# Encoder layer with PEER experts, one core: 48 late tokens leave the feature matmuls in place of 32

## The reference, cut to what matters

```python
def peer_layer(x, w_q, keys1, keys2, u_tab, v_tab):
    q = (xt @ w_q).reshape(T, PEER_HEADS, 2, half)
    s1 = jnp.einsum('thd,hnd->thn', q[:, :, 0], keys1)
    s2 = jnp.einsum('thd,hnd->thn', q[:, :, 1], keys2)
    v1, i1 = lax.top_k(s1, PEER_TOPK)
    v2, i2 = lax.top_k(s2, PEER_TOPK)
    ...                                  # the 16 best of v1 + v2: eidx, sc
    gate = jax.nn.softmax(sc, axis=-1)
    u = jnp.take(u_tab, eidx, axis=0)
    a = jnp.einsum('nhkd,nd->nhk', u, x)             # "features"
    w = jax.nn.gelu(a, approximate=False) * gate
    return jnp.einsum('nhk,nhkd->nd', w, jnp.take(v_tab, eidx, axis=0))
x = layer_norm(DN_ALPHA * x + peer_layer(x, ...), ln2_g, ln2_b)
```

## Time and profile before

| | |
|---|---|
| timed executions | 1432.85, 1434.01, 1437.87 us, median 1434.01 |
| profiled execution | 1433.48 us, its span 1431.8 us |
| TensorE, VectorE, GpSimd, ScalarE busy | 98%, 76%, 63%, 42% of the span |
| feature matmuls (three lines, 128 tiles) | 3072 of 352 columns |
| features begin, sums begin | 349.16 us, 893.5 us |
| DMA in the 60 us from 700, in the 100 us from 1000 | 416 GB/s, 369 GB/s |

### The profile page before, as it was taken

How to read it: one execution, slowest core, us unless ns; L and a number is a source line. 1 busy time by engine, 2 the same in 40 slices (tenths; PEclk the granted TensorE clock), 3 DMA queues, 4 the chain that set the end, 5 groups by cost and what they waited for, 6 DMA issues and landing times.

```text
span 1431.8 us, 24761 instructions
## 1 busy us (share of the span) xinstructions
PE 1406.7 (98%) x8045; PEld 1248.2 (87%) x8045; DVE 1087.3 (76%) x2324; ACT 606.7 (42%) x1019; POOL 903.4 (63%) x595
## 2 busy tenths in 40 slices
PE   9999999999999999999999999999999999999996
PEld 5888878888999999999999999878888888888885
DVE  5366666688999998858774885987777777777786
ACT  5666751324333354454544443333333333333332
POOL 3422331335599978979888786766666666666744
PEclk9999999999999999999999999999999999999998
DMA  6213120423689979999999899999999999999981
GB/s 243 75 50 113 59 90 1 147 84 102 197 316 342 323 259 395 417 389 418 418 417 399 341 381 407 383 388 387 371 374 374 372 366 360 367 368 366 372 315 59
DMA packets 138959, 415.41 MB, mean 290 GB/s; under 512 B 13904, under 2 KB 56656, under 8 KB 136720
## 3 DMA queue, kind: packets, MB, share of 16 engines
q1 hardware_dynamic: 80128, 240.69, 45.9%
q0 software_dynamic: 42064, 151.15, 26.8%
q10 hardware_dynamic: 16704, 22.81, 4.3%
HBM read 363.89 MB, written 50.14 MB: 289 GB/s over the span
## 4 chain that ended last, share of the span: by engine, by line
PE 76%; DVE 8%; DMA 5%; POOL 4%; issue 3%; ACT 2%; SPq 1%; DVEq 0%; ACTq 0%; POOLq 0%
PE banks L2019 12%; PE banks L2021 11%; PE banks L2020 11%; PE banks L1964 11%; PE banks L1965 11%; PE banks L1966 11%; DMA raw<-v_tab 3%; POOL lo L501 2%; PE banks L2081 2%; PE banks L2237 1%; PE banks L2238 1%; POOL rows L822 1%; PE banks L2174 1%; DMA rows<-u_rows,expert_at 1%; DVE rows L1454 1%
## 5 line engine op out<-in xcount | busy, mean ns | idle before, releaser
L501 POOL TENSOR_TENSOR lo<-raw,hi 128x1024 fp32r<-128x1024 f32 x224 | 540.2, 2413 | 416.5 <-ACT hi L495 396.5
L1964 PE MATMUL banks<-x1T_hi,hi 128*128 128x352 f32 (+3 forms) x1168 | 389.9, 334 | 1.3 <-ACT kept L1106 1.0
L1965 PE MATMUL banks<-x1T_lo,hi 128*128 128x352 f32 (+3 forms) x1168 | 384.6, 329 | 0.0
L1966 PE MATMUL banks<-x1T_hi,lo 128*128 128x352 f32 (+3 forms) x1168 | 383.6, 328 | 0.0
L495 ACT ACTIVATE hi<-raw 128x1024 fp32r<-128x1024 f32 x291 | 305.6, 1050 | 57.0 <-DMA raw<-u_t 37.4
L2019 PE MATMUL banks<-hi,wgt_hi 128*128 128x512 f32 x750 | 292.1, 389 | 2.0 <-DVE wgt_lo L1811 1.9
L2020 PE MATMUL banks<-lo,wgt_hi 128*128 128x512 f32 x750 | 291.8, 389 | 0.0
L2021 PE MATMUL banks<-hi,wgt_lo 128*128 128x512 f32 x750 | 291.8, 389 | 0.0
L1964 PEld LDWEIGHTS banks<-x1T_hi,hi 128*128 128x128 f32 x1168 | 219.8, 188 | 6.2 <-ACT kept L1106 1.3
L1966 PEld LDWEIGHTS banks<-x1T_hi,lo 128*128 128x128 f32 x1168 | 220.3, 189 | 4.4
L1965 PEld LDWEIGHTS banks<-x1T_lo,hi 128*128 128x128 f32 x1168 | 220.1, 188 | 3.9
(11 more groups left out here) (245 smaller groups left out, 1846.7 us busy)
## 6 DMA issues: line engine op xcount, KB each, us to landing
raw<-u_t SPq DMA_DIRECT2D x128, 512.0 KB
raw<-v_tab SPq DMA_DIRECT2D x128, 512.0 KB
g_scratch<-stage SPq DMA_DIRECT2D x12, 2048.0 KB
gelu_scratch<-gelu ACTq DMA_DIRECT2D x116, 192.0 KB
ga<-gelu_scratch SPq DMA_DIRECT2D x29, 768.0 KB
gg<-g_scratch SPq DMA_DIRECT2D x14, 1536.0 KB
raw<-w SPq DMA_DIRECT2D x26, 512.0 KB
raw<-w_pq SPq DMA_DIRECT2D x16, 512.0 KB
```

The costliest lines, as they stand in the source:

```text
L501: eng.tensor_tensor(l[:, :], raw[:, c % RAW_SLOTS, :], h[:, :].bitcast(F32), ALU.subtract).then_inc(odd_lo_ready if by_vector(c) else lo_r ...
L1964: pe.matmul(o, h[:, s], hiT[:, k, tokens], start=(k == 0), stop=False)
L1965: pe.matmul(o, h[:, s], loT[:, k, tokens], start=False, stop=False)
L1966: ins = pe.matmul(o, l[:, s], hiT[:, k, tokens], start=False, stop=(k == KT - 1))
```

## The change

The late tokens are 48 and not 32, as a set of 32 (the last ones) and a set of 16. The feature matmuls have 336 columns and not 352, and gelu scratch in DRAM has 336 columns. The late tokens need 48 gathers and not 32. The number of u rows gathered in the feature phase stays 144, because 16 more rows of block 0 (`EXTRA` 32) go into the sums, where octets 2 to 5 take three each and the other octets up to 13 two; their gelu and gates are applied in two batches. Expert numbers, gates and weights of the late tokens are turned by way of DRAM, two stores and two loads each, and the second set's x goes through DRAM too (eight copies) and gets a home of its own: VectorE and ScalarE change homes four times in place of three. Six groups in the last pair are scattered in three parts, and not four. The chosen experts are turned one tile later (`CHOSEN_AT`), the gathers for late tokens start one tile later (`LATE_ROWS`), the first 16 late dots are spread differently (`FIRST_DOTS`). The 1.0 in the columns past the dense ones is written into the two load buffers `ga` once, and not into the gelu buffers. A load of gelu scratch now fills 336 of 384 columns of each of four rows of a partition. Four `gelu` buffers of 336 columns and `small` with 192 columns keep the buffers behind them at multiples of 256 bytes.

```diff
-LATE_TOKENS = 32
-SPREAD = P // LATE_TOKENS
+LATE_SETS = (32, 16)
+LATE_TOKENS = sum(LATE_SETS)
 LATE_AT = P - LATE_TOKENS
-LATE_RANKS = RANKS // SPREAD
+LATE_RANKS = sum(RANKS // (P // n) for n in LATE_SETS)
+LATE_MOVES = len(LATE_SETS)
 FEATURED = DENSE - LATE_TOKENS
-EXTRA = 16
+EXTRA = 32
+EXTRA_BATCHES = (16, 16)
...
-LATE_ROWS = (0, 0, 0, 2, 3, 3, 2, 2, 2, 2, 2, 2)
+LATE_ROWS = (0, 0, 0, 0, 2, 3, 3, 3, 3, 2, 2, 2)
+FIRST_DOTS = (0, 2, 2, 2, 2, 3, 2, 3)
+assert sum(FIRST_DOTS) == 2 * ROWS
...
+CHOSEN_AT = 1
+FIRST_BATCH_AT = 8
...
-    a_dram = nc.dram_tensor("gelu_scratch", (ETILES // 4, P, 4, DENSE), F32, kind="Internal").ap()
+    a_dram = nc.dram_tensor("gelu_scratch", (ETILES // 4, P, 4, FEATURED), F32, kind="Internal").ap()
+    turn_dram = [[nc.dram_tensor(f"{what}_scratch{i}", (P // n, n, n), dt, kind="Internal").ap()
+                  for i, n in enumerate(LATE_SETS)]
+                 for what, dt in (("late_number", U32), ("late_gate", F32), ("late_weight", F32))]
+    second_dram = nc.dram_tensor("second_scratch", (P // LATE_SETS[1], LATE_SETS[1], D), F32, kind="Internal").ap()
...
+        idle_gelu = ExitStack()
+        extra.append(sb("extra2", [P, D], F32, idle_gelu))
+        idle_gelu.close()
+        gelu = [sb(f"gelu{i}", [P, FEATURED]) for i in range(GELU_SLOTS)]
...
-        small = sb("small", [P, P])
+        small = sb("small", [P, P + 64])
...
-        late_parts = row_weight[:, LATE_TOKENS:].bitcast(BF16).rearrange("p (m t two) -> p m t two", m=3, two=2)
+        late_parts = sel[:, 0, :, :].rearrange("p b n -> p (b n)")[:, 0:3 * LATE_TOKENS].bitcast(BF16).rearrange(
+            "p (m t two) -> p m t two", m=3, two=2)
+        late_x_second = sel[:, 0:2, :, :].rearrange("p m b n -> p (m b n)")
...
-            used_by = n // 2 if n < len(late_slots) else WHOLE_GROUPS + (n - len(late_slots)) // 3
+            if n < len(late_slots):
+                used_by = n // 2 - (HOT_SLOTS if n // 2 >= WHOLE_GROUPS else 0)
+            else:
+                used_by = WHOLE_GROUPS + (n - len(late_slots)) // 3
...
-        EXTRA_ASKED_AT, EXTRA_DOT_AT = (2, 4), (5, 7)
-        def extra_rows(j, par, at):
-            if isinstance(j, int) and j == 0:
-                return {k: (2 * par + i, i) for i, k in enumerate(at)}
-            return {at[1]: (2 * j + (2 + par), par)}
+        ASKED_AT = {2: (2, 4), 3: (0, 2, 4)}
+        DOT_AT = {2: (4, 6), 3: (2, 4, 6)}
+        def extra_number_of(i, each, q):
+            return (2 * i + (EXTRA_BATCHES[0] - 12 + q) if each == 2 else 3 * i + (q - 2)) if not early_extras(i) else 2 * i + q
...
+            sp.dma_start(second_dram.rearrange("g t d -> t g d"),
+                         x1[LATE_AT:LATE_AT + LATE_SETS[1], TB - 1, :].unsqueeze(1).to_broadcast(
+                             [LATE_SETS[1], P // LATE_SETS[1], D])).then_inc(second_stored, 16)
...
+            def store_numbers():
                 sp.wait_ge(late_numbers_ready, 1)
-                for g in range(SPREAD):
-                    sp.dma_start(late_numbers[late_group(g), :],
-                                 block_numbers[LATE_AT:, late_group(g)]).then_inc(late_numbers_moved, 16)
-            def move_gates():
+                for i, n, tokens, columns in late_sets():
+                    sp.dma_start(turn_dram[0][i].rearrange("g t c -> t g c"),
+                                 block_numbers[tokens, :].rearrange("t (g c) -> t g c", c=n)
+                                 ).then_inc(late_numbers_stored, 16)
+            def load_numbers():
+                sp.wait_ge(late_numbers_stored, 16 * LATE_MOVES)
+                for i, n, tokens, columns in late_sets():
+                    sp.dma_start(late_numbers[:, columns], turn_dram[0][i].rearrange("g t c -> (g t) c")
...
+            def load_second_x():
+                sp.wait_ge(selT_ready, 2)
+                sp.wait_ge(second_stored, 16)
+                sp.dma_start(late_x_second, second_dram.rearrange("g t d -> (g t) d")).then_inc(second_x_moved, 16)
...
+                    if first and t == 6:
+                        load_gates_turned()
+                    if first and t == 8:
+                        load_second_x()
+                    if weights and t == 0:
+                        store_weights()
+                    if weights and t == 2:
+                        load_weights()
...
-            for k in range(2):
+            for k in range(3):
                 load_features(k, A_PRE // 4 - 1)
-            move_numbers()
-            for k in range(2, 4):
-                load_features(k, A_PRE // 4 - 1)
+            store_numbers()
+            load_features(3, A_PRE // 4 - 1)
+            load_numbers()
             two_chunks(0, first=True)
             two_chunks(1)
             two_chunks(2)
-            move_weights()
-            with sp.Fori(3, O_MID) as o:
-                two_chunks(o)
+            two_chunks(3)
+            two_chunks(4, weights=True)
...
-                    sp.dma_start(ga[slot][:, :, :], a_dram[g]).then_inc(comb_loaded[slot], 16)
+                    sp.dma_start(ga[slot][:, :, 0:FEATURED], a_dram[g]).then_inc(comb_loaded[slot], 16)
...
+                    if k in ASKED_AT[each]:
+                        q = ASKED_AT[each].index(k)
+                        extra_number(extra_number_of(2 * j + par, each, q), q)
                     first = U_ROWS + par * ROWS + k + AHEAD
                     gather(v_rows, [first, first + 1], o, (S_V + 8 * par + k, 2 * o))
-                    if k in extras:
-                        extra_row(extras[k][1])
+                    if k in ASKED_AT[each]:
+                        extra_row(q)
...
+            v_octet(0, 0, 2)
+            v_octet(0, 1, 2)
+            for slot in range(GELU_SLOTS):
+                pool.wait_ge(gelu_stored[slot], 16 * (A_PRE + A_MID) // GELU_SLOTS)
+            with pool.Fori(1, 3) as i:
+                v_octet(i, 0, 3)
+                v_octet(i, 1, 3)
+            with pool.Fori(3, OCTETS // 2 - 1) as i:
+                v_octet(i, 0, 2)
+                v_octet(i, 1, 2)
...
-                act.activation(gelu[k][:, 0:FEATURED] if keep is None else kept[:, keep, 0:FEATURED],
+                act.activation(gelu[k][:, :] if keep is None else kept[:, keep, 0:FEATURED],
...
+            def second_home():
+                act.wait_ge(second_x_moved, 16)
+                act.wait_ge(row_used, R_PRE * ROWS + LATE_SETS[0])
+                home(late_x_second)
...
-                        if first and tile == 0:
+                        if first and tile == CHOSEN_AT:
...
                         if second and tile == 0:
+                            second_home()
+                        if third and tile == 0:
...
-            for slot in range(GELU_SLOTS):
-                dve.memset(gelu[slot][:, FEATURED:DENSE], 1.0).then_inc(ones_ready, 1)
...
+                    if homes is not None and tile == 0:
+                        dve.wait_ge(homes_ready, homes)
+                    done = sum(FIRST_DOTS[:tile]) if first else 2 * tile
+                    for n in range(done, done + (FIRST_DOTS[tile] if first else 2)):
...
-            two_chunks(0, first=True)
+            two_chunks(0, homes=3, first=True)
             two_chunks(1)
-            two_chunks(2, second=True)
+            two_chunks(2, homes=4)
+            two_chunks(3, homes=5)
...
+            for slot in range(2):
+                dve.memset(ga[slot][:, :, FEATURED:DENSE], 1.0).then_inc(ones_ready, 1)
...
+                    if k in DOT_AT[each]:
+                        q = DOT_AT[each].index(k)
+                        n = extra_number_of(i, each, q)
+                        extra_dot_of(n, q, i + 1 if q < 2 else i - 1)
...
+            def weigh_extras(batch):
+                dve.wait_ge(dots_gelu_ready, 2 + batch)
+                weigh_rows(slice(FIRST_EXTRA + sum(EXTRA_BATCHES[:batch]),
+                                 FIRST_EXTRA + sum(EXTRA_BATCHES[:batch + 1]))).then_inc(row_weight_ready, 1)
+                dve.wait_ge(row_weight_ready, 2 + batch)
```

More of the change, by code:

```diff
@@ L647, in two_chunks @@
+            def two_chunks(o, first=False, weights=False):
                 for t in range(MID_TILES):
@@ L1109, in gelu_tile @@
                 if keep is None:
-                    if first and k == 0:
-                        act.wait_ge(ones_ready, GELU_SLOTS)
                     act.wait_ge(gelu_ready, 4 * it + (k + 1))
@@ L1750, in _, with two_chunks @@
             one_hots(0, 0, True)
-            def two_chunks(o, first=False, second=False, last=False):
+            def two_chunks(o, homes=None, first=False, last=False):
                 for tile in range(8):
```

150 lines of the change are left out of this document (86 added, 64 removed).

## The result

The changed kernel takes 1441.51 us, the median of 7 runs (1437.50 to 1443.99), the kernel before 1434.01 in its 7 runs: a ratio of 1.0051, 95% interval 1.0030 to 1.0072. It is slower by 7.5 us, where 1427.5 was forecast, and lies above the range. The profiled execution took 1438.85 us, 5.4 more than that of before.

A forecast was written before the change was run, and what follows sets the result against it. TensorE, busy for 98% of the span, was taken as the bound. Gains and losses of 1.4 + 7.4 - 0.3 - 2.5 = 6.0 us took the profiled 1433.48 us to 1427.5 us, range 1419 to 1439.

The forecast's parts named there:

- Term 1: Feature matmuls: 16 columns fewer gain 0.157 us a tile, 20.1 us over all 128 tiles; bounds nothing and 22.5 us.
- Terms 2 and 3: Up to the first scatter, and late numbers by way of DRAM: together one gain, 1.4 us, with GpSimd as bound.
- the side chance named: Before the first scatter: a 2.30 us conversion may take 1 us or less, bringing the scatter 1.3 us earlier.
- Term 4: Feature tiles 57 to 103: 47 x 0.157 = 7.4 us gained, with DMA transfers fitting.
- The second stop of VectorE: Tiles 57 to 103: second late-token block adds a 9.8 us stop, GpSimd's lead falls to about 2 us, costed at nothing.
- The turned gates, weights and x lie beside other work: Feature phase: nobody waits for these moves within a pair of chunks, so they cost nothing.
- the mean over a pair: Over a pair of chunks: DMA needs 50.3 us at 416 GB/s, TensorE 51.9 us, so it fits by 1.6 us.
- Term 5: Last pair of chunks: 3.8 us gained, 0.9 lost to more matmuls, 3.2 to waiting for VectorE's products: -0.3 us.
- Term 6: Expert sums: 16 more row gathers cost 1.5 us there and 1 us at their start; bounds 0 and 15.
- The rival that held for slower: Expert sums become DMA-bound: loss of 14 us and not 2.5, total 1439.0 us; chance 0.14.
- One or two more dots on VectorE in the 32.7 us of an octet fit: Expert sums: VectorE, busy for three quarters, could take two more dots even at 3.29 us.
- The 1 us that the sum put at the start of the sums: Where the expert sums begin, with the feature stretch's DMA behind them: a loss of 1 us.

The follow-up runs named there:

- q3: Kernel before with 336-column feature matmuls and gelu (16 tokens' gelu left out) and the gates' parts in PSUM, nothing else added: 1422.15 us.
- c2: Changed kernel with each extra dot cut from 1024 columns to 64, gathers whole: 1432.07 us, ratio 0.9987.
- t5: Changed kernel with extra dots on odd tiles in octets with two, and only two of three late products made on VectorE: 1428.03 us.
- p2: Changed kernel with gates' parts in PSUM, extra dots on odd tiles in octets with two, second x loaded in the second pair of chunks: 1426.24 us.
- a1: Changed kernel with the second x's load moved from the first pair of chunks into the second: 1440.38 us, ratio 1.0046.
- c1: Changed kernel with the extra rows' dots one tile later in each octet, on odd tiles: 1441.53 us, ratio 1.0051.
- d1: Changed kernel with extra dots on odd tiles (5 and 7) in octets with two, unchanged in octets with three: 1436.56 us, ratio 1.0002.
- d2: As d1, and the second x is loaded in the second pair of chunks: 1434.06 us, ratio 0.9998.
- p1: Changed kernel with the three parts of the 48 late tokens' gates copied once into PSUM and read from there: 1432.08 us, ratio 0.9990.
- q2: Changed kernel with gates' parts in PSUM and extra dots on odd tiles, second x loaded where the change put it: 1427.95 us.
- a2: As a1, with the turned gates' storing and loading also moved into the second pair of chunks: 1444.27 us, ratio 1.0072.
- p3: Kernel before with the parts of its 32 late tokens' gates in PSUM: 1431.93 us, ratio 0.9984.

## Why the prediction was wrong

**Term 1** was about right: tiles 3 to 12 gain 0.19 us each, a little above the upper bound (22.5 us over 128 tiles, 0.176), and tiles 60 to 102 0.155, where 0.157 was forecast. What it can bring to the end is another thing: 12.7 us in q3, of some 20.

**Terms 2 and 3** were right. Waits for low halves at tiles 14 to 20 sum to 2.6 us (forecast about 3). The scatter starts at 530.16, which is the side chance named, since the conversion took 0.55 us and not 2.30. GpSimd goes on at 526.36 (forecast 526.4), tile 57 starts at 577.73 (forecast 578.0). The lines of VectorE and GpSimd, for the earlier trace rows:

```profile
524.99 0.55 DVE L1757 CAST gate_hi<-selT 128x768 f16<-128x768 f32 x1
```

```profile
526.36 0.21 POOL L886 COPY expert_at<-small 128x8 uint32<-128x8 uint32 x1 [7.06 <-DMA small<-late_number_scratch]
```

**Term 4** was 7.4 us; U57 to U104 brought 2.7. The rate was right from U60 on, and 416 GB/s held. The second stop of VectorE came (for the earlier trace rows: 14.1 us at the longest), GpSimd's lead fell to 1.6 us, and it cost nothing, as forecast. "The turned gates, weights and x lie beside other work: nobody waits for them" failed: the feature loads share the transfers with them. Tile 59 was issued at 568.1 in both kernels and landed at 580.3, not 576.3. ScalarE's halves wait for such loads, the stage copies stand behind them, and TensorE's scatter waits for those:

```profile
575.01 1.06 ACT L518 ACTIVATE hi<-raw 128x1024 fp32r<-128x1024 f32 x1 [7.16 <-issue]
...
580.29 1.06 ACT L518 ACTIVATE hi<-raw 128x1024 fp32r<-128x1024 f32 x1 [2.91 <-DMA raw<-u_t]
```

The first line is the half of tile 58, whose load was issued at 563.3 in both kernels; the half began at 572.88 before. Its bracket names no releaser.

I had checked the mean over a pair (it fits by 1.6 us) and not the moment. The size is partly the clock's: in 580 to 590 us it was granted 0.83 in the changed kernel, c2, t5 and p2, which lost 3.3 to 4.1 us between U57 and U60, and 1.00 in a1, c1, d1, d2, p1 and q2, which lost 0.8 to 1.4. In the first four TensorE had waited 2.0 to 2.9 us in front of that scatter, in the other six 1.1 to 1.7.

**Term 5** was the step that cost most: 0.3 us of loss forecast, 3.8 measured. (Term 4 was off by more in the profiled execution, 4.4 us, but moving its loads won nothing that can be told, and moving term 5's operand won 9.4.) The price of a product was about right (1.35 us against 1.55), the mechanism too. Wrong was to count only VectorE's own 3.2 us for the last scatter. GpSimd, kept back by the dots that queue behind the products (it waited 5.9 us for them from 795 to 885, and 2.9 in p1), was only 0.8 us ahead of its old times (the subtraction at 829.04 began at 829.88 before), TensorE 4.6, so TensorE met it at tiles 114 to 123; then came a wait of 3.5 us for ScalarE and the lower clock. Without the long products TensorE wins 4 us in the same stretch. The Trainium skill (SBUF — State Buffer, "SBUF: two separate sides") says that whichever of the two starts first holds the port pair for its whole instruction. In the expert sums the trace agrees: 0.55 or 2.73 us for one instruction, by who came first (over all traces, 809 of 816 of VectorE's products and subtractions of weights that began ahead of a subtraction of GpSimd took about 0.55). For the late products the starts in the trace do not bear it out: the product at 803.16 began 0.32 us ahead of GpSimd's subtraction and took 3.28 us, while the subtraction took its usual 2.40, and of the 32 such products in all traces that began 0.3 to 0.4 us ahead, 31 took 3.3. So a start shortly ahead of GpSimd's does not protect them, and why is not shown. What the runs do show is the way out: 0.68 us for every product once one input is in PSUM.

**Term 6** forecast 2.5 us; 5.1 were lost after V0, and all for another reason. The rival that held for slower (transfers, 1439.0) gave nearly the right time by a mechanism that did not occur: four octets with three extra rows ran at shares of 0.97 to 1.04 without loss. "One or two more dots on VectorE in the 32.7 us of an octet fit" failed, although they fit in sum: VectorE is 78% busy. What failed is the order, two dots in front of weights that TensorE waits for. I had not costed that move of the dots from odd to even tiles at all: it stood in the sum at nothing, without a reason. The 1 us that the sum put at the start of the sums did not come: from V0 to V18 the kernel won 1.5.

By the profiled executions the misses are 4.4 (tile 104 at -4.4, not -8.8), 3.5 (term 5: 3.8, not 0.3), 2.6 (term 6: 5.1, not 2.5) and 0.9 behind the last matmul: 11.4 us, from 1427.5 to 1438.9.

The pieces of 1344 bytes cost about what they carry. The queue that stores to the gelu scratch moved 12.5% fewer bytes in as many packets, and its share fell from 4.3 to 3.8%: a piece of 1536 bytes took 65.2 ns on average and one of 1344 takes 58.3. The loads of the scratch were 3712 pieces of 6144 bytes at 254 ns each and are 14848 of 1344 at 59.2 ns, in all 6.8% less.

In medians: the 15.3 us from the changed kernel to p2 are 9.4 for the parts in PSUM and 5.8 for the dots and the second x together, of which q2 against p1 gives 4.1 to the dots, and d1 against the changed kernel 5.0. For the second x the three pairs that differ by it give 1.1 (a1), 2.5 (d2) and 1.7 us (p2), none of them clear of the intervals. What the added parts still cost then is 4.1 us, p2 against q3.

Open stays why the loads of the gates and of the second x, 24 and 512 KB, delay a feature load by 4 us; they were always moved with something else ahead or behind, and were not made smaller one by one. That a lower clock follows the longer waits of TensorE at this place is what the rows show, and no run was made to test it. Open is also why the loss in the octets with three dots runs from nothing (the changed kernel, a2, d2) to 6.6 us (c1) between V18 and V69.

## What to carry to other kernels

When the bound engine gets faster, ask of each engine behind it how much earlier its own work becomes, not how busy it is: here GpSimd came 0.8 us earlier where TensorE came 4.6. Before adding VectorE work with two inputs in SBUF beside a busy GpSimd, see whether one input can live in PSUM (here 9.4 us for one copy), and if not, let the instruction that meets GpSimd be one that nobody waits for. Time a change also with such collisions removed: this one costs 7.5 us with them and gains 5.7 without (p2 against p3).

## What the hardware showed that I had not expected

- 0.24 us decide over 2.2: a subtraction of 384 columns took 0.55 or 2.73 us by whether it or GpSimd's began first, and a kernel loses about 1 us an octet or nothing by it. What happens far ahead of the place seems enough to turn it: the changed kernel, a1, a2 and p1 have the same program in the sums, and lose 0, 3.4, 0 and 3.6 us in the same octets with three dots.
- It works both ways. The extra dot at 1176.69 began first and ended at 1177.90, and GpSimd's subtraction of 1177.60 took 2.56 us in place of 2.40.
- Runs of one kernel spread unevenly: p1 ran from 1426.2 to 1439.1 us and d1 from 1430.1 to 1439.4, p2 from 1423.5 to 1429.5. The meetings may have a part in it, but that isn't shown: a2 has them too and ran from 1442.3 to 1445.8.
- A DMA share of 1.04 (412 GB/s) held for 30 us of the sums twice, with no wait of TensorE.
